# Expert outputs scattered through DRAM: seven of eight expert pairs leave TensorE's scatter for GpSimd's indirect DMA

## What is computed

```python
g_idx = jnp.argmax(g_prob, axis=-1)                      # best of 4 groups
top_v, top_i = lax.top_k(e_logits, TOP_K_IN_GROUP)       # 2 of its 4 experts
e_w = jax.nn.softmax(top_v, axis=-1) * g_w
gate = jnp.sum(jax.nn.one_hot(expert, N_EXPERTS) * e_w[..., None], axis=1)
hg = jnp.einsum('td,edf->tef', t, w1)
hu = jnp.einsum('td,edf->tef', t, w3)
a = jax.nn.silu(hg) * hu * gate[..., None]
y = jnp.einsum('tef,efd->td', a, w2)                     # 16 experts, hidden size 512
```

## Time and profile before

| what | value |
|---|---|
| median of 3 runs | 862.55 us (861.58 to 865.38) |
| the profiled execution's own time | 866.96 us |
| its span, first to last instruction | 865.2 us |
| TensorE (PE) busy | 809.6 us, 94% |
| DVE, ScalarE, GpSimd busy | 225.9, 161.8, 24.1 us |
| mean granted TensorE clock | 0.955 |
| HBM read, written | 276.20 MB, 1.18 MB |

### The profile page before, as it was taken

The page is one execution under the profiler, slowest core; times in us unless marked ns, Lnnn a source line. Parts: engine busy times, 40 slices in busy tenths (PEclk is TensorE's granted clock), DMA queues, the critical chain, the costliest instruction groups (busy, mean ns, idle before and its releaser), DMA issues.

```text
span 865.2 us, 10983 instructions
## 1 busy us (share of the span) xinstructions
PE 809.6 (94%) x4403; PEld 472.1 (55%) x4403; DVE 225.9 (26%) x617; ACT 161.8 (19%) x372; POOL 24.1 (3%) x45
## 2 busy tenths in 40 slices
PE   4799879999999999999799999999997989999996
PEld 4387458755454545453588667755445345444533
DVE  2301231521110111111699631521111111111105
ACT  2110231420000000001405852520000000000012
POOL 5023000000000000000000000000000000000000
PEclk9799899889999999999999999889998999999997
DMA  9996994968999999999915589728999108999931
GB/s 294 387 381 232 390 334 170 430 248 351 430 416 425 425 429 426 428 426 399 387 54 193 195 302 377 293 84 348 432 423 420 47 20 354 428 425 420 427 164 52
DMA packets 52133, 278.27 MB, mean 322 GB/s; under 512 B 2615, under 2 KB 4099, under 8 KB 39778
## 3 DMA queue, kind: packets, MB, share of 16 engines
q1 hardware_dynamic: 50800, 275.78, 79.5%
q10 hardware_dynamic: 770, 1.05, 0.4%
q0 software_dynamic: 496, 0.55, 0.3%
HBM read 276.20 MB, written 1.18 MB: 321 GB/s over the span
## 4 chain that ended last, share of the span: by engine, by line
PE 88%; DMA 5%; DVE 3%; issue 2%; SPq 1%; ACT 1%; POOL 1%; DVEq 0%; POOLq 0%
PE ps L460 85%; DMA ring<-in_w_ada 5%; SPq L422 1%; PE ps L711 1%; PE ps L828 1%; PE ps L689 1%; DVE rstd L1323 1%; DVE work L1545 0%; POOL work L1241 0%; ACT hT L1015 0%; PE ps L608 0%; DVE hT L1731 0%; PE ps L946 0%; ACT root L1003 0%; DVE hT L1334 0%
## 5 line engine op out<-in xcount | busy, mean ns | idle before, releaser
L460 PE MATMUL ps<-ring,work 128*64 128x512 f32 x1488 | 361.3, 595 | 0.1
L460 PEld LDWEIGHTS ps<-ring,work 128*64 128x64 f32 x1488 | 113.2, 137 | 177.8 <-issue 175.8
L460 PE MATMUL ps<-hT,ring 128*128 128x256 f32 x656 | 147.8, 388 | 6.9 <-ACT hT L1015 5.0
L460 PEld LDWEIGHTS ps<-hT,ring 128*128 128x128 f32 x656 | 126.5, 195 | 28.5 <-issue 7.6
L460 PE MATMUL ps<-work,xtok 128*128 128x128 f32 x576 | 78.3, 295 | 9.6 <-issue 6.5
L460 PEld LDWEIGHTS ps<-work,xtok 128*128 128x128 f32 x576 | 73.8, 208 | 21.9 <-issue 21.9
L460 PE MATMUL ps<-spare,work 128*64 128x512 f32 x144 | 65.6, 598 | 1.8 <-DVE work L1524 1.8
L460 PE MATMUL ps<-work 128*128 128x256 f32 x272 | 63.3, 386 | 0.0
L460 PEld LDWEIGHTS ps<-work 128*128 128x128 f32 x272 | 50.3, 190 | 19.9 <-issue 13.8
L1545 DVE TENSOR_TENSOR work<-work,ps 128x256 f32<-128x256 f32 x34 | 19.3, 611 | 158.5 <-PE ps L460 158.5
L1695 DVE SCALAR_TENSOR_TENSOR work<-work,dw 128x256 f32<-128x256 f32 x120 | 50.8, 480 | 1.0
(11 more groups left out here) (214 smaller groups left out, 484.6 us busy)
## 6 DMA issues: line engine op xcount, KB each, us to landing
ring<-in_moe_w SPq DMA_DIRECT2D x88, 2048.0 KB, 13.8
ring<-in_w_ada SPq DMA_DIRECT2D x21, 2048.0 KB, 15.9
spare<-in_moe_w SPq DMA_DIRECT2D x8, 2048.0 KB, 19.4
ring<-in_conv_w SPq DMA_DIRECT2D x6, 2048.0 KB, 14.7
spare<-in_w_ada SPq DMA_DIRECT2D x3, 2048.0 KB, 12.6
ring<-in_w_in_ab SPq DMA_DIRECT2D x2, 2048.0 KB, 20.2
ring<-in_w_out_ab SPq DMA_DIRECT2D x2, 2048.0 KB, 18.4
ring<-in_w_in_ab SPq DMA_DIRECT2D x1, 1024.0 KB, 18.0
```

The source lines that it names most:

```text
L460: return nc.tensor.matmul(out, lhsT, rhs, start=start, stop=stop, skip_group_check=True)
```

## The change

For the first seven pairs of each layer (`SENT`), the scatter matmuls and the transposes of `pick_gate` go. Instead two matmuls of 128x4 (`pick` times `send`) give each slot its gate weight and its row number in a DRAM table `yrows` of 512 rows of 4 KB: token number, plus 256 for the token's second choice. DVE brings these to `row_at` and `row_gate`; the evictions of `ysel` multiply by `row_gate`; GpSimd writes `ysel` by an indirect DMA to the named rows (`send_rows`). A slot without a token has a number past the table's end, which `bounds_check` drops. After the seventh pair GpSimd reads the table back in four DMAs of 128 rows (`fetch_rows`), 2 MB in all, into `ysum` (the buffer `xtok`) and `yadd` (the buffer `sq`); DVE adds the two (`sum_sent`), and TensorE adds the sum to `psx` by 2 times 8 matmuls against the identity (`add_sent`): the first 8 ahead of the last pair's `w2` products, the other 8 behind them. The last pair and the second round of a crowded pair keep their scatter. Both tables are filled with zeros once, by two DMAs of 2 MB that GpSimd issues right after the pooling of layer 0.

```diff
+            pool.wait_ge(s_xt, 4)
+            nc.gpsimd.memset(xtok[:, 0, :], 0.0).then_inc(zero_ready, 1)
+            pool.wait_ge(zero_ready, 1)
+            for l in range(2):
+                pool.dma_start(yrows[l].rearrange("(p k) d -> p k d", k=ROWS // P),
+                               xtok[:, 0:1, :].to_broadcast([P, ROWS // P, D])).then_inc(s_zero, 16)
+            pool.wait_ge(s_zero, 32)
+            def send_rows(l):
+                for i in range(SENT):
+                    n = i + l * PAIRS
+                    pool.wait_ge(ysel_lo[0], n + 1)
+                    pool.wait_ge(ysel_hi[0], n + 1)
+                    nc.gpsimd.indirect_dma_start(yrows[l], IndirectOffsetOnAxis(ap=row_at[n % 2][:, 0:1], axis=0),
+                                                 ysel, None, bounds_check=ROWS - 1,
+                                                 oob_is_err=False).then_inc(y_sent, 16)
+            def fetch_rows(l):
+                pool.wait_ge(ss_done, 2 * l + 2)
+                pool.wait_ge(spread_done[0], (l + 1) * PAIRS)
+                pool.wait_ge(y_sent, 16 * SENT * (l + 1))
+                for g in range(2):
+                    for c, dst in enumerate((ysum, yadd)):
+                        a = c * NT + g * TG
+                        pool.dma_start(dst[:, g, :], yrows[l][a:a + TG, :]).then_inc(y_back[g], 16)
...
+            def add_sent(l, g):
+                pe.wait_ge(y_zeroed, l + 1)
+                pe.wait_ge(y_summed, 2 * l + g + 1)
+                for m in range(DC):
+                    mm(psx[:, m, g * TG:(g + 1) * TG], ysum[:, g, m * P:(m + 1) * P], ident, False, True)
...
+                if sent:
+                    return
+                if r == 0:
+                    add_sent(l, 1)
                 pe.wait_ge(y_zeroed, l + 1)
                 pe.wait_ge(ysel_lo[r], n + 1)
                 for m in range(DC):
...
+                if r == 0 and i == SENT:
+                    sum_sent(l, 0)
                 dve.wait_ge(turn_done[r], n * 2 + 2)
                 V.tensor_copy(hidT[:, 2:4, :], ps[:, 7, 0:2 * P].rearrange("p (f j) -> p f j", f=2)).then_inc(
                     hidT_hi[r], 1)
```

More of the change, by code:

```diff
@@ L13 @@
 from concourse import mybir
+from concourse.bass import IndirectOffsetOnAxis
 P = 128
@@ L62 @@
 PAIRS = NE // 2
+SENT = PAIRS - 1
 CAP = 64
@@ L245, in backbone @@
         rs = sb("rs", [P, 12, 2])
-        gate = sb("gate", [P, 2, NE + 2])
+        send = sb("send", [P, 2, 2, NE])
+        target, gate = send[:, :, 0, :], send[:, :, 1, :]
+        row_gate = sb("row_gate", [P, 1])
+        row_at = [sb(f"row_at{n}", [P, 1], mybir.dt.int32) for n in range(2)]
         slot = sb("slot", [P, 2, NE + 2])
@@ L339, in backbone @@
         htok_ready = sem("htok_ready")
-        pick_ready = [sem(f"pick_ready_round{r}") for r in range(2)]
+        gates_ready = sem("gates_ready")
+        s_zero = sem("s_zero")
+        zero_ready = sem("zero_ready")
+        y_sent = sem("y_sent")
+        y_back = [sem(f"y_back{g}") for g in range(2)]
+        y_summed = sem("y_summed")
         spread_done = [sem(f"spread_done_round{r}") for r in range(2)]
@@ L671, in compact @@
                 ahead = r == 0 and i + 1 < PAIRS
+                sent = r == 0 and i < SENT
                 for w, bank, j in ((w1, 6, 0), (w3, 7, 2)):
@@ L686, in compact @@
                             pe.wait_ge(hsel_hi[r], n + 1)
-                            pe.wait_ge(pick_ready[r], n + (l + 1 if r == 0 else 1))
+                            pe.wait_ge(gates_ready, l + 1)
+                            if not sent:
+                                for g in range(2):
+                                    nc.tensor.transpose(ps[:, 7, g * TG:(g + 1) * TG], pick[:, g, :], ident)
                             for g in range(2):
-                                last = nc.tensor.transpose(ps[:, 7, g * TG:(g + 1) * TG], pick_gate[:, g, :], ident)
+                                last = mm(ps[:, 7, NT:NT + 4].rearrange("p (s u) -> p s u", s=2), pick[:, g, :],
+                                          send[:, g, :, 2 * i:2 * i + 2], g == 0, g == 1)
                             last.then_inc(spread_done[r], 1)
@@ L715, in compact @@
                 if ahead:
+                    pe.wait_ge(ysel_hi[0], n)
                     gather(0, 1)
+                elif r == 0:
+                    add_sent(l, 0)
                 tile_landed(l, i, 4)
@@ L1772, in shape_constants @@
     t[:, C_QUAD:C_QUAD + P // QUAD] = np.tile(np.eye(P // QUAD, dtype=np.float32), (QUAD, 1))
+    for g in range(2):
+        t[:, C_TOKEN + g] = g * TG + tok - NOWHERE
     for w, size in enumerate(WINDOWS):
@@ L1799 @@
     args.append(nc.dram_tensor("in_shape_consts", (P, C_W), F32, kind="ExternalInput").ap())
+    args.append([nc.dram_tensor(f"yrows{l}", (ROWS, D), F32, kind="Internal").ap() for l in range(2)])
     for name, shape in OUTPUTS:
```

113 lines of the change are left out of this document (73 added, 40 removed).

## The result

The changed kernel takes **885.93 us** (median of 4 runs, 885.36 to 890.95) against 862.07 us for the kernel before on the same chip (4 runs, 860.1 to 865.38): ratio 1.0258, 95% interval 1.0219 to 1.0297. It is slower, as forecast, by 23.9 us where 14.6 were forecast: above the forecast's own range of 870 to 883, and within the wider one of 862 to 890.

The account below looks back on a forecast made before the run. TensorE and the DMA weight stream were both taken as full; zero fill 7.4, layer 0 7.0 and layer 1 0.2 us sum to 14.6 us on the 862.55 us median: 877.1 us, range 870 to 883.

Parts of the forecast that it names:

- three signs of being wrong: Landings near sends still 4.9 us apart; TensorE's tile wait near 112 us not grown; last pair waiting for DVE's sum.
- The double bound: In the expert pairs, TensorE (29.27 us a pair) and the weight stream (29.4 us for six tiles) are both full.
- TensorE's saving: In the sent expert pairs, removed scatters and transposes save TensorE 3.5 us each, worth only the slack of the tiles.
- The zero fill: Before layer 0's experts, filling 4.19 MB delays the weight queue and a `w_ada` tile TensorE waits for: +7.4 us.
- The sends: Rows sent in the expert pairs delay the last tile: 4.5 us in layer 0, 2.6 in layer 1.
- Dropped slots still move: Rival, chance 0.10: all 128 rows of each send are written, 4.5 us more in layer 0, about 3.9 in layer 1: 885.5 us.
- The read-back: In each layer's last pair, reading 2.10 MB ahead of the `w2` tiles' landing delays the last tile by 5.1 us.
- From `w2` to the end: Last pair: 10.74 us before, 12.74 with the second `add_sent` (2.0 us); the first hides in the tile wait.
- the round trip stalls the last pair: Rival, chance 0.08: send, reads and sum outlast the last tile's wait; legs 4 us longer cost 5 us a layer: 887 us.
- Layer 1's: Layer 1's experts: saving nearly cancelled by sends, read-back and additions, ending at 848.0 against 847.85: +0.2 us.
- Bytes ride free: Rival, chance 0.12: zero fill, stores and read-back use hidden gaps of the DMA engines, -12.2 us together: 850.3 us.

Follow-up runs that it names:

- no send: The changed kernel without the indirect writes, their semaphore raised directly by GpSimd; zero fill, read-back and additions stay: 878.36 us, ratio 1.0145.
- neither: The changed kernel without zero fill, indirect writes, read-back, sums and additions, so only TensorE's part of the change is left: 854.73 us, ratio 0.9891.
- both mends: The changed kernel with the zero fill issued later and the sums and additions moved behind the last pair's `w2` products: 872.30 us, ratio 1.0090.
- the two pairs with later additions: The kernel before, sending only layer 1's first two pairs, with sums behind the fourth pair and additions ahead of the fifth: 865.32 us, ratio 0.9996.
- late fill: The changed kernel with the two zero fills issued only after TensorE's pooling product, some 50 us later: 882.71 us, ratio 1.0197.
- additions behind: The changed kernel with both sums behind DVE's copy of hidT and both halves of `add_sent` behind the last pair's `w2`: 882.05 us, ratio 1.0188.
- all dropped: The changed kernel with the `row_at` offset past the table, so the bounds check drops all 128 slots of each send: 883.82 us, ratio 1.0200.
- reads only: The changed kernel with sends and read-back but without DVE's sums and TensorE's additions: 872.02 us, ratio 1.0064.

## Why the prediction was right, and where its sizes were off

The time lies 8.8 us above the forecast of 877.1 and outside its own range. The direction and the mechanism (two full resources, each added byte charged) held; of the terms, that for the additions failed, that for the read-back was too large, and in layer 1 the two errors cancelled.

Of the prediction's three signs of being wrong, the third came in full: the last pair waits for DVE's sum and not for a tile (the row at 413.66). The other two came in part. The single wait at the `w_ada` tile did not grow, though the tile came 6.3 us later; and next to the sends that landed at 279.2 and 338.6 in layer 0 the tiles' landings stayed 4.9 us apart, while near those of 250.5, 369.8 and 398.6 one gap each was 5.4 to 5.7.

*The double bound* held. Pairs of 25.8 us of TensorE's work take 29.4 and more; in the kernel without sends or fetch the tile of layer 0 is no earlier (+0.2 against the -1 forecast). TensorE's saving, -4.6 in layer 0 (1 of gaps, 3.6 of slack) and -9.5 in layer 1 (4.9 and 4.6) by the forecast's terms, measured -3.3 and -10.1.

*The zero fill*: +7.4 forecast, 8.2 by the means above. Its sign in the trace was partly wrong: not one long wait but several.

*The sends*: +4.5 in layer 0, measured 4.5 on the tile (228.2 - 223.7) and 5.2 on the layer; +2.6 in layer 1, measured 0.9. *Dropped slots still move* fell.

*The read-back* was mis-sized: +5.1 on the last tile, measured 1.8 with sends (230.0 - 228.2) and 2.5 without. The step said that it takes a third of the engines ahead of the tile; but the last tile landed at 410.54 and the reads at 409.4 to 416.3, so a good part of the bytes moved after it, at the cost of the next stage: its first tile landed 239.2 us after the gather, 233.6 without the fetch. The Trainium skill (DMA: Bandwidth & Descriptors, "SWDGE vs HWDGE vs iDMA") says that GpSimd's transfers and the hardware queues' go to different internal queues of each engine, which takes turns between them. The rows agree: of GpSimd's reads, issued 12.5 us and more behind the last expert tile, the first landed 1.1 us before it and the others 1.7 to 5.8 us after it, and the tile came later for them.

*From `w2` to the end* is the step that failed: "The first `add_sent` is in the wait for the tile and costs nothing; without that cover it would cost 2.0." It had no cover, and it cost 6.8 us from the tile's landing to `w2` (410.54 to 417.34): 3.1 of wait and 3.7 for matmuls at the half clock. In the rival's own count, from the seventh pair's `w2` end (386.25): the first sum was done after 27.3 us where 22.5 were forecast, and the tile landed after 24.3 where 27.5 were. The send leg was too short in the sum, 10.6 us from issue to landing (7.3 assumed); the reads, 13.1 from the first issue to the first sum, were as forecast. By its own condition ("slack 3.0") the rival *the round trip stalls the last pair* had come about in part: it was a share of the truth and not the whole, since the forecast's other terms stood. The forecast allowed up to 3 us a layer for the half clock, as an upper margin, and left it out of the sum; between the layers, where it had nothing, the profile has +2.3, with a granted clock of 0.75 in the second ten microseconds there, against 0.88 before:

```profile
439.90:449.90 10.00, 10.00 (x37) 8.32 (x36) 6.73 (x24) 5.01 (x14) 0.00 (x0) 0.75 0.96 356
```
```profile
423.80:433.80 10.00, 10.00 (x43) 8.56 (x42) 7.81 (x25) 4.95 (x13) 0.00 (x0) 0.88 1.05 384
```

This is no fixed part of the change. The stretch takes 150.6 to 150.7 us in five of the kernels (before, no send, neither, both mends, the two pairs with later additions), with 0.87 or 0.88 in those ten microseconds, and 153.0 to 153.1 in five (as changed, late fill, additions behind, all dropped, reads only), with 0.74 to 0.76; without the fetch it is 152.3 and 0.83. The kernel with both mends has all of the change's work and takes 150.6. What decides between the two is open.

*Layer 1's* +0.2 is met to the tenth by accident: the terms for bytes were 4.7 us too high (2.6 + 5.1 against 0.9 + 2.1) and those for the additions 5.3 too low (2.0 against 7.3). That is luck. *Bytes ride free* fell: sends and reads cost 7.8 us in layer 0.

Left open: why the start before layer 0 spreads over 6.6 us between executions of kernels that are alike there, what sets the time between the layers, how the additions' 7 us a layer split into their work and their place, and how much of the place is clock and how much wait.

## What to carry to other kernels

Before work is taken from the busiest engine, look whether the stream that feeds it is also full in the same window; then a saving is worth the slack at the last transfer and no more, and each byte added is charged. Work placed "into the wait" for a transfer is only hidden if its own input is there before the wait begins; otherwise put it behind, and judge a round trip by landings under the load of that place, not by the smallest transfer in the trace. An idle wait of TensorE can be paid a second time in its clock: here the 3.0 and 3.8 us were followed by 0.57 and 0.55, while waits of 2.4 and 2.1 were followed once by 1.00 and once by 0.62.

## What the runs showed of the hardware

An indirect send of 128 slots keeps GpSimd for 1.0 us, and lands after 10.0 to 12.4 us in a full stream; with nothing to move it still took 9.9 for the one looked at. The Trainium skill's formula (DMA: Bandwidth & Descriptors, "Anatomy of one DMA — SWDGE (gpsimd) path"), 2.0 us plus bytes at 436 GB/s, would give an estimate of 2.6 us for 61 rows of 4 KB; these rows, under the full stream, disagree, as the forecast's 5.6 us for a tiny load did. Slots that the bounds check drops cost no bytes in the queue (8.95 MB against 8.94), though the HBM line of the profile's page counts them. Behind a deep stream of weights a read of 0.5 MB took up to 28.5 us to land.
